# Two transformer blocks in sequence: residual with tokens on partitions, norms by token and by half of the tokens, gate/up/down interleaved, first product by k tiles

## The reference

```
for l in range(2):                                    # first block
    mod = silu(c) @ ada_w[l] + ada_b[l]               # shift, scale, gate for mixer and feed-forward
    h = rms_norm(x, g_pre_mix[l]) * (1.0 + scale_m) + shift_m
    proj = h @ w_in[l] + b_in[l]                      # 1024 -> 1280: q, k, v, u
    mix = concat([attention(q, k, v), pool(u)]) @ w_out[l]
    x = x + gate_m * rms_norm(mix, g_post_mix[l])
    h = rms_norm(x, g_pre_ffn[l]) * (1.0 + scale_f) + shift_f
    f = (silu(h @ w_gate[l]) * (h @ w_up[l])) @ w_down[l]      # 1024 -> 2816 -> 1024
    x = x + gate_f * rms_norm(f, g_post_ffn[l])
for l in range(2):                                    # second block
    z = rmsnorm(x, attn_norm[l]) @ w_in[l]            # split in 12 parts for the three mixers
    x = x + concat([y_a, y_b, y_c]) @ w_out[l]
    u = rmsnorm(x, ffn_norm[l]) @ ffn_w_up[l]
    x = x + (silu(causal_conv3(u[:, :FF])) * u[:, FF:]) @ ffn_w_down[l]
return rmsnorm(x, final_norm)
```

## Time and profile before

| | us |
|---|---|
| runs | 1308.36, 1308.45, 1309.59 |
| median | 1308.45 |
| span of the profiled execution | 1307.2 |
| TensorE busy | 1200.2 |
| VectorE busy | 878.0 |
| ScalarE busy | 625.0 |
| GpSimd busy | 30.2 |
| moved by DMA | 248.66 MB, 190 GB/s on average |

### The profile page before, as it was taken

How to read it: one execution, slowest core, us unless ns; L and a number is a source line. 1 busy time by engine, 2 the same in 40 slices (tenths; PEclk the granted TensorE clock), 3 DMA queues, 4 the chain that set the end, 5 groups by cost and what they waited for, 6 DMA issues and landing times.

```text
span 1307.2 us, 22230 instructions
## 1 busy us (share of the span) xinstructions
PE 1200.2 (92%) x9456; PEld 1154.1 (88%) x9456; DVE 878.0 (67%) x1355; ACT 625.0 (48%) x990; POOL 30.2 (2%) x32
## 2 busy tenths in 40 slices
PE   2589799989889899999899989999999998999997
PEld 1578699989878799999889789999989888999997
DVE  6697888876567566664377557888446655788743
ACT  2434544443345454453355556556435556555631
POOL 5400000000000000000000000000000000000000
PEclk9699999999989899999999999999999999999999
DMA  8863498887422345665243235556434423555630
GB/s 338 327 251 157 189 332 325 340 327 292 156 106 105 129 176 215 249 238 182 96 149 131 96 130 185 183 185 237 178 99 148 161 97 130 183 183 187 251 134 33
DMA packets 33570, 248.66 MB, mean 190 GB/s; under 512 B 3744, under 2 KB 4032, under 8 KB 6080
## 3 DMA queue, kind: packets, MB, share of 16 engines
q1 hardware_dynamic: 32400, 243.94, 51.3%
q10 hardware_dynamic: 720, 2.10, 0.4%
q0 software_dynamic: 352, 1.20, 0.4%
HBM read 246.18 MB, written 1.05 MB: 189 GB/s over the span
## 4 chain that ended last, share of the span: by engine, by line
PE 78%; DVE 12%; DMA 5%; ACT 5%; issue 1%; DVEq 0%; ACTq 0%
PE bank L440 24%; PE bank L442 23%; PE bank L441 23%; DMA raw_w<-weights 4%; DVE lo_w L1141 4%; PE bank L447 3%; DVE raw_w L1159 2%; PE bank L459 2%; ACT hi_w L867 2%; PE bank L748 2%; DVE raw L1168 1%; DVE prob L1218 1%; DVE smax L1221 1%; PE bank L728 1%; DMA c_row<-c 1%
## 5 line engine op out<-in xcount | busy, mean ns | idle before, releaser
L440 PE MATMUL bank<-in_hi,lo_w 128*128 128x256 f32 x1984 | 569.5, 287 | 43.5 <-DVE in_lo L1177 22.0
L1141 DVE TENSOR_TENSOR lo_w<-raw_w,hi_w 128x1024 fp32r<-128x1024 f32 (+4 forms) x344 | 426.0, 1279 | 205.1 <-ACT hi_w L867 205.0
L441 PE MATMUL bank<-in_lo,hi_w 128*128 128x256 f32 x1984 | 560.4, 282 | 0.0
L442 PE MATMUL bank<-in_hi,hi_w 128*128 128x256 f32 x1984 | 560.2, 282 | 0.0
L867 ACT ACTIVATE hi_w<-raw_w 128x1024 fp32r<-128x1024 f32 (+4 forms) x344 | 360.5, 1097 | 211.9 <-PE bank L442 177.9
L440 PEld LDWEIGHTS bank<-in_hi,lo_w 128*128 128x128 f32 x1984 | 379.8, 191 | 54.6 <-issue 39.7
L441 PEld LDWEIGHTS bank<-in_lo,hi_w 128*128 128x128 f32 x1984 | 380.4, 192 | 0.9 <-issue 0.5
L442 PEld LDWEIGHTS bank<-in_hi,hi_w 128*128 128x128 f32 x1984 | 379.8, 191 | 0.0
L440 PE MATMUL bank<-hid_hi,lo_w 128*128 128x256 f32 x704 | 200.1, 284 | 4.6 <-DVE hid_lo L1473 4.6
L442 PE MATMUL bank<-hid_hi,hi_w 128*128 128x256 f32 x704 | 198.0, 281 | 0.0
L441 PE MATMUL bank<-hid_lo,hi_w 128*128 128x256 f32 x704 | 198.0, 281 | 0.0
(11 more groups left out here) (174 smaller groups left out, 1121.1 us busy)
## 6 DMA issues: line engine op xcount, KB each, us to landing
raw_w<-weights SPq DMA_DIRECT2D x174, 1024.0 KB, 5.0
raw_w<-weights SPq DMA_DIRECT2D x32, 1408.0 KB, 6.1
raw_w<-weights SPq DMA_DIRECT2D x4, 1280.0 KB, 5.6
raw_w<-weights SPq DMA_DIRECT2D x8, 512.0 KB, 3.6
const<-const_table SPq DMA_DIRECT2D x1, 2434.0 KB, 13.1
raw_w<-weights SPq DMA_DIRECT2D x2, 1152.0 KB, 5.2
x<-x_t ACTq DMA_DIRECT2D x1, 1024.0 KB, 16.1
out_t<-raw SPq DMA_DIRECT2D x4, 256.0 KB, 2.5
```

The lines of the kernel that those rows point to most:

```text
L440: nc.tensor.matmul(o, st[1], mv[0], start=start, stop=False, **kw)
L441: nc.tensor.matmul(o, st[0], mv[1], start=False, stop=False, **kw)
L442: return nc.tensor.matmul(o, st[0], mv[0], start=False, stop=stop, **kw)
L1141: nc.vector.tensor_tensor(lo_w[:, m % NSPLIT, cut], raw_view(unit)[:, cut], hi_w[:, m % NSPLIT, cut].bitcast(F32), ALU.subtract).then_inc( ...
```

## The change

Everything is rewritten around a new layout of the residual; what is computed stays the same.

- `x` is now [128, 2, 1024]: tokens on partitions, in two halves T of 128 tokens. A norm is a sum along a row: ScalarE's square with an accumulated sum (`root`), with no matmul. The normed tokens go through TensorE as transposes (`turn_norm`, eight of 128x128 per half), and the high and low parts of the result are taken from PSUM. Gains, shifts and gates are now rows over all partitions; those of the modulation are computed as columns, written to memory and read back as rows by GpSimd (`mod_row`), which also multiplies by the scale row in three norms (`scale`).
- The out-projection and the down product have the activations stationary and 512 columns of weights moving (`into_y`). A `wd` unit is now two k tiles of all 1024 columns, 11 per layer, and the results stay in four banks of PSUM.
- A `wd` unit stands behind each pair of `gu` units (`ffn_units`), and only a ring of six hidden tiles is kept.
- A stage ends by halves (`ending`, `chain`): the last two units are finished for the first half of tokens, then for the second; the next stage's first two units are multiplied token half by token half (`front`), as soon as that half is normed. For gate/up these two units are turned back by eight transposes each.
- The input product of layer 0 goes by k tiles (`ink`, 128 rows of all 1280 columns), between the `ada` units that make shift and scale of the same tiles; the product takes six banks at once. In layers 0 and 1 q and k are rotated with tokens on partitions and then transposed; in layers 2 and 3 the same holds for the latents, and the unit `z` 2 has 208 columns in the place of padded and doubled blocks.
- `NSPLIT` is 3, raw slots have 2048 columns, and the `ada` units have other places.

```diff
-SLOT = FF
-NSPLIT = 2
+SLOT = 2048
+NSPLIT = 3
+RING = 6
...
+ADA_AFTER = {
+    ("wo", 0, 2): [(0, 8), (0, 9), (0, 10)], ("wo", 0, 3): [(0, 11), (0, 16), (0, 17)],
+    ("wo", 0, 0): [(0, 18), (0, 19), (0, 12)], ("wo", 0, 1): [(0, 13), (0, 14), (0, 15)],
+}
...
+def ffn_units(L):
+    lag = 1 if L < 2 else 2
+    units = []
+    for i in range(FT // 2):
+        units += [("gu", L, 2 * i), ("gu", L, 2 * i + 1)]
+        if i >= lag:
+            units.append(("wd", L, i - lag))
+    return units + [("wd", L, w) for w in range(WD - lag, WD)]
...
+    for j in range(4):
+        for n in (4 + j, j):
+            units.append((("ada", 0, n), *SHAPES["ada"]))
+        add("ink", 0, 2 * j)
+        add("ink", 0, 2 * j + 1)
...
-    def sums(N, tiles, ones, src, wait):
-        job = ("sums", *N)
-        b = take(job)
-        for i, t in enumerate(tiles):
-            wait(t)
-            last = nc.tensor.matmul(b[:, 0:256], ones, src[:, t, :], start=(i == 0), stop=(i == len(tiles) - 1))
-        last.then_inc(*sig(*job))
...
+    def turn_norm(N, T):
+        for c in range(2):
+            pe.wait_ge(*due("normed", N, T, c))
+            transposes(("tr", N, T, c), [normed[:, 512 * c + P * i:512 * c + P * (i + 1)] for i in range(4)])
...
+    def into_y(L, w, unit, T, first=False, last=False, before_second=None):
+        wait, slot, src = (mixed_wait, down_wait)[w](L)
+        wt = weights(unit, ("y", L, w, T, 1) if last else ("used", unit))
+        for c in range(2):
+            if c and before_second is not None:
+                before_second()
+            job = ("y", L, w, T, c)
+            if first:
+                take(job, 4 * w + 2 * T + c)
+            for n in range(2):
+                t = 2 * unit[2] + n
+                wait(t)
+                done = exact(ps(job)[:, :], [half(v_[:, slot(t), :], T) for v_ in src], [v_[:, n, cols(c)] for v_ in wt],
+                             start=(first and n == 0), stop=(last and n == 1))
+            if last:
+                done.then_inc(*sig(*job))
+        if T == 1 and not last:
+            done.then_inc(*sig("used", unit))
+    def ending(L, w, one, other, front):
+        N = after(L, w)
+        into_y(L, w, one, 0)
+        into_y(L, w, other, 0, last=True)
+        into_y(L, w, one, 1)
+        if N[0] == "final":
+            into_y(L, w, other, 1, last=True)
+            return
+        banks(*((4, 5, 6, 7) if w == 0 else (0, 1, 2, 3)))
+        if L >= 2:
+            into_y(L, w, other, 1, last=True, before_second=lambda: turn_norm(N, 0))
+        else:
+            into_y(L, w, other, 1, last=True)
+            turn_norm(N, 0)
+        front(0)
+        turn_norm(N, 1)
+        front(1)
...
+    def front(name, N, L, units):
+        def run(T):
+            job = (name, L, T)
+            b = take(job)
+            for i, u in enumerate(units):
+                done = tokens(two(b, i), u, ("used", u) if i == 0 else (name, L, 1), T,
+                              wait=lambda t: pe.wait_ge(*due("in_lo", N, T, t // 4)))
+                if i == 0 and T == 1:
+                    done.then_inc(*sig("used", u))
+            done.then_inc(*sig(*job))
+        return run
...
+            for kk in range(6):
+                for T, c in places:
+                    done = slice_of(kk, T, c)
+                done.then_inc(*sig("used", ("ink", 0, kk)))
...
+    def mod_row(L, kind, w):
+        n = ROWS[(L, kind, w)]
+        pool.wait_ge(*due("modcol", L, kind, w))
+        pool.dma_start(mod_rows[n, :].rearrange("(t p) -> p t", p=P), modcol[:, n, :], allow_slow_non_contiguous=True).then_inc(*sig("row_out", n, by=16))
+        pool.wait_ge(*due("row_out", n))
+        slot = ("gate", "scale", "shift").index(kind)
+        load(rows[:, slot, :], mod_rows[n:n + 1, :], D, f"row{slot}", L, kind, w)
...
+    def scale(N, L, w):
+        for T in range(2):
+            for c in range(2):
+                pool.wait_ge(*due("x", L, w, T, c))
+                if T == 0 and c == 0:
+                    pool.wait_ge(*due("row1", N[1], "scale", 0 if N[0] == "mix" else 1))
+                if T == 1:
+                    pool.wait_ge(*due("normed", N, 0, c))
+                nc.gpsimd.tensor_tensor(scaled[:, cols(c)], x[:, T, cols(c)], rows[:, 1, cols(c)], ALU.mult).then_inc(
+                    *sig("scaled", N, T, c))
...
+    def root(name, key, T, i, wait, src):
+        for c in range(2):
+            sc.wait_ge(*wait(c))
+            nc.scalar.activation(junk[:, :], src(c), ACT.Square, accum_out=ssq[:, T, c:c + 1]).then_inc(*sig("squared", *key, T, c))
+            if c == 0:
+                sc.wait_ge(*due("squared", *key, T, 0))
+                nc.scalar.activation(sbias[:, T, :], ssq[:, T, 0:1], ACT.Identity, bias=k("eps"), scale=1.0 / D).then_inc(*sig("sbias", *key, T))
+        sc.wait_ge(*due("sbias", *key, T))
+        sc.wait_ge(*due("squared", *key, T, 1))
+        r = tok_rstd[:, T, i:i + 1]
+        nc.scalar.activation(r, ssq[:, T, 1:2], ACT.Ln, bias=sbias[:, T, :], scale=1.0 / D).then_inc(*sig("mean_log", *key, T))
+        sc.wait_ge(*due("mean_log", *key, T))
+        nc.scalar.activation(r, r, ACT.Exp, scale=-0.5).then_inc(*sig(name, *key, T))
+    def chain(L, w, T, following):
+        N = after(L, w)
+        if L < 2:
+            root("rstd_post", (L, w), T, 0, lambda c: due("y", L, w, T, c), lambda c: ps(("y", L, w, T, c))[:, :])
+        root("rstd", (N,), T, 1, lambda c: due("x", L, w, T, c), lambda c: x[:, T, cols(c)])
+        if following is None:
+            return
+        prepare(following, (0,))
+        for c in range(2):
+            copy(("tr", N, T, c), in_hi[:, 4 * c:4 * c + 4, P * T:P * (T + 1)], by_tile(ps(("tr", N, T, c))), "in_hi", N, T, c, frees=False)
+        prepare(following, (1,))
...
+    def residual(L, w, T):
+        if L >= 2:
+            for c in range(2):
+                job = ("y", L, w, T, c)
+                ve.wait_ge(*due(*job))
+                nc.vector.tensor_tensor(x[:, T, cols(c)], x[:, T, cols(c)], ps(job)[:, :], ALU.add).then_inc(*sig("x", *job[1:], frees=job))
+            return
+        ve.wait_ge(*due("row0", L, "gate", w))
+        for c in range(2):
+            job = ("y", L, w, T, c)
+            ve.wait_ge(*due("squared", L, w, T, c))
+            if T == 1:
+                ve.wait_ge(*due("x", L, w, 0, c))
+            nc.vector.tensor_tensor(gained[:, cols(c)], ps(job)[:, :], rows[:, 0, cols(c)], ALU.mult).then_inc(*sig("gained", *job))
+        ve.wait_ge(*due("rstd_post", L, w, T))
+        for c in range(2):
+            job = ("y", L, w, T, c)
+            ve.wait_ge(*due("gained", *job))
+            nc.vector.scalar_tensor_tensor(x[:, T, cols(c)], gained[:, cols(c)], tok_rstd[:, T, 0:1], x[:, T, cols(c)], ALU.mult, ALU.add).then_inc(
+                *sig("x", *job[1:], frees=job))
+    def norm(N, T):
+        ve.wait_ge(*due("rstd", N, T))
+        r = tok_rstd[:, T, 1:2]
+        for c in range(2):
+            dst = final[:, T, cols(c)] if N[0] == "final" else normed[:, cols(c)]
+            if T == 1 and N[0] != "final":
+                ve.wait_ge(*due("tr", N, 0, c))
+            if N == ("mix", 0):
+                ins = nc.vector.tensor_scalar(dst, x[:, T, cols(c)], r, None, ALU.mult)
+            elif modulated(N):
+                ve.wait_ge(*due("scaled", N, T, c))
+                ve.wait_ge(*due("row2", N[1], "shift", 0 if N[0] == "mix" else 1))
+                ins = nc.vector.scalar_tensor_tensor(dst, scaled[:, cols(c)], r, rows[:, 2, cols(c)], ALU.mult, ALU.add)
+            else:
+                row, _ = norm_row(N)
+                ve.wait_ge(*due("row2" if N[0] == "ffn" else "row1", "norm", N))
+                ins = nc.vector.scalar_tensor_tensor(dst, x[:, T, cols(c)], r, row[:, cols(c)], ALU.mult, ALU.mult)
+            ins.then_inc(*sig("normed", N, T, c))
...
+    def chain(L, w, T, following):
+        N = after(L, w)
+        residual(L, w, T)
+        norm(N, T)
+        if following is None:
+            return
+        lo(following, (0,))
+        for c in range(2):
+            ve.wait_ge(*due("in_hi", N, T, c))
+            s_ = slice(P * T, P * (T + 1))
+            nc.vector.tensor_tensor(in_lo[:, 4 * c:4 * c + 4, s_], by_tile(ps(("tr", N, T, c))[:, :]), in_hi[:, 4 * c:4 * c + 4, s_].bitcast(F32),
+                                    ALU.subtract).then_inc(*sig("in_lo", N, T, c, frees=("tr", N, T, c)))
+        lo(following, (1,))
+        behind(following)
```

More of the change, by code:

```diff
@@ L38 @@
 POOLS = (2, 4, 8, 16)
-SLOT = FF
+SLOT = 2048
 NRAW = 3
-NSPLIT = 2
-NADA = 24
+NSPLIT = 3
+RING = 6
+PAIRED = [h for j in range(4) for h in (j, j + 4)]
 def const_table():
@@ L476, in product @@
                         wait(t)
+                    if between is not None and (i, t) == (1, 0):
+                        between()
                     c = c0 + P * i
                     kw = {} if wait is None or n == 1 else {"skip_group_check": True}
```

(49 more changed lines are left out.)

1940 lines of the change are left out of this document (1032 added, 908 removed).

## The result

The changed kernel takes 1289.2 us (median of four runs, 1284.4 to 1290.1), against 1308.9 us for the kernel before on the same chip: a ratio of 0.984 (95% interval 0.981 to 0.986). It is faster, by 19.6 us or 1.6%; forecast were 44 us. The profiled execution has a span of 1287.8 us.

What follows compares the result with a forecast made beforehand. The prediction took TensorE, busy 92% of 1307.2 us, as the bound. Stage times summed to 1248 us, plus 15 for the clock gave a 1263 span, and 1264 us kernel time, 44 less; range 1236 to 1291.

Steps and rivals of the forecast that it cites:

- the clock term: Six waits in layers 0 and 1, each followed by 2 to 3 us of half speed: 15 us added.
- Layer 0 to the input product of layer 1: From layer 0's out-projection to layer 1's input product: reached at 340 us, 363.3 before, including 14 us of stage-end waits.
- The upper bound of 24 us: Layer 0's shift row: longest assumed transfer through memory, four times pool_w's 6.1 us; the lower bound was 4.5.
- DMA stays under its rate: 312 GB/s: Gate/up/down stage: 5.2 MB in 16.8 us, where before held 309 GB/s without starving.
- TensorE's stream: Whole kernel: ones matmuls, rotations and padded columns go, 208 transposes come; net 41 us less work.
- 3 + 3.7: Stage ends in layers 0 and 1: TensorE waits 3 us for the first token half, 3.7 for the second.
- 306.7: Layers 2 and 3: us per layer, against 320.2 and 317.9 before; TensorE's last product ends at 1241.6.
- The 208 columns: Rival, unit z 2: 208-column steps fall back to plain fp32 at 0.365 us, 26 us more, 1289; chance 0.20.
- the fixed cost per matmul: Rival: 1536 wide steps replace 3072 narrow ones, saving 10 ns each; 15 us less, 1249; chance 0.04.
- The clock did not stay low: Answers a rival: split stage ends and softmax loops leave 1.2 GHz stretches, 108 us lost, 1356; chance 0.08.
- The cheap chains: Rival: waits in softmax, layer 0 and stage ends halve because ScalarE and VectorE overlap better; 1240; chance 0.10.
- The round trip rival: Rival, modulation row writes: 24 us instead of 5.4 each, layer 0's chain waits 19 longer; 1283; chance 0.06.

Runs made afterwards that it cites:

- fast writes: Against the changed kernel: modulation weights, biases and gains packed so each row is written in 32-byte runs and read in natural order; 1253.8 us, ratio 0.957.
- the run that was to confirm it: Against the changed kernel: rows read at once from the norm rows, 4-byte-element writes issued behind and not waited for until the last; 1295.8 us.

## Why the prediction was right and wrong

The starts of stages as forecast (without the clock term), in the kernel after, and in the one with fast writes:

| start of | forecast | after | fast writes |
|---|---|---|---|
| first product | 26 | 25.3 | 25.2 |
| out-projection, layer 0 | 104 | 111.5 | 110.4 |
| turned tokens, layer 0's stage end | 141 | 160.8 | 146.8 |
| input product, layer 1 | 340 | 372.2 | 345.0 |
| out-projection, layer 1 | 394.8 | 442.7 | 404.4 |
| first product, layer 2 | 625.2 | 665.2 | 627.9 |
| span | 1248 (+15) | 1287.8 | 1251.0 |

**The step that failed** is in "Layer 0 to the input product of layer 1": the row's way through memory at 5.4 + 4.5 us, taken near pool_w's 6.1 "with as many runs". pool_w is a read in runs of 512 bytes; its number of runs was like, their length was not. Measured: 9.0 to 15.4 us of waiting for the write, 8.4 for the read. The upper bound of 24 us held, but the rival made from it had only the latency in layer 0. Its 1283 lies near the measured 1289 by luck: most of the loss has another reason. Between the kernel after and the one with fast writes the span differs by 36.8 us: 1.0 before layer 0's out-projection, 13.0 from there to its first gate/up product (4.8 because the shift column is made later, its units having waited for transfers, 6.7 from the longer write, the rest from the read), 13.2 from there to layer 1's input product, 11.1 in layer 1's input product and attention, and -1.5 behind. So by the places where TensorE waits some 8 us are latency, which I had the form of, and about 28 are **disturbance of the weight transfers**, which the forecast had nowhere. That the writes in short runs cost 35 us is shown by the runs; the split into 8 and 28 is read from the traces, and the run that was to confirm it left the latency in the read. The sentence "DMA stays under its rate: 312 GB/s" was true of bytes: with fast writes this stage moves 301 GB/s and no wait of TensorE for weights is left in it. It said nothing of short writes on the same engines.

**What held.** TensorE's stream: 41 us less work forecast, 45 less busy, busy 1155.2 in the forecast's 1140 to 1160. First product at 25.3 (26). Layers 2 and 3 and the end, 622.6 (623). Layer 1's part from its out-projection to layer 2's first product, 222.5 (230.4): the forecast was too dear there, since the waits at its first stage end are 1.17 + 1.49 + 1.17 = 3.8 us and not 3 + 3.7. The 3 came from a chain "8.6 us" long, and the sum is wrong: without GpSimd's scalings and the transposes its parts are 9.0 us, with them over 13, and nothing says which of them overlap.

**Terms that were off and cancelled.** In the sum of layers 2 and 3 two times 306.7 from 625.2 end at 1238.6, where the text goes on with 1241.6; 306.7 holds one of the two stage ends of 3 us that the text names, and 1241.6 holds layer 2's other one. The start to layer 0's out-projection takes 6 to 7 us longer than 104, with VectorE waiting 7.9 us for rounded weights between 25 and 111 us, which my list of VectorE's work didn't have. The clock term of 15 us is not seen on top: with fast writes the span is 1251.0, 3 from the 1248 without it. Its granted clock in the windows is 0.98 in layer 0's gate/up/down stage and 0.88 in layer 1's attention, so some of the loss is there, and the smaller waits at stage ends will have paid for it. I can't split the two further, and that the sum without the clock comes so near is in part luck.

**The rivals.** The 208 columns (0.20) and the fixed cost per matmul (0.04) fall by the timeline of the kernel after. A step of 208 columns takes 0.11 us, not 0.365, and one of 512 still 0.23:

```profile
443.22 0.39 PE L476 MATMUL bank<-hi_w,in_hi 128*128 128x512 f32 x1
443.45 0.39 PE L474 MATMUL bank<-hi_w,in_lo 128*128 128x512 f32 x1
443.69 0.39 PE L475 MATMUL bank<-lo_w,in_hi 128*128 128x512 f32 x1
...
679.87 0.26 PE L474 MATMUL bank<-hi_w,in_lo 128*128 128x208 f32 x1
679.97 0.27 PE L475 MATMUL bank<-lo_w,in_hi 128*128 128x208 f32 x1
680.08 0.27 PE L476 MATMUL bank<-hi_w,in_hi 128*128 128x208 f32 x1
```

The Trainium skill's rule of a fixed cost per matmul ("TensorE: Matmul & The Clock Gate", section "Wait — 56ns, not 53.3ns?") is not borne out here: at a granted clock of 1.00 what lies above the columns at 2.4 GHz is 10 ns for 256 columns, 20 for 512 and 24 for 208. The 15 us that the prediction put beside this rule come from the 10 ns of the rows; by the figure of about 2.5 ns per matmul that this section of the Trainium skill gives, the estimate is 4 us. The clock did not stay low: 1.00 from layer 1's out-projection on. The cheap chains (0.10) were right for layer 1's first stage end, 3.8 us of waits in the place of 6.7, but even the kernel with fast writes ends at 1251 and not near their 1240. The round trip rival (0.06) was the right place at far too low a chance: it was the only term whose two bounds (4.5 and 24) lay a factor of five apart, and the rows could not narrow it.

## What to carry to other kernels

The price of a small write is set by its contiguous runs and not by its bytes: the same 4 KB in 1024 runs of 4 bytes or in 128 of 32. Whether the number of runs or their length counts, no run here separates; pool_w, a read in 1024 runs of 512 bytes, landed in 6.1 us in the kernel before and in 9.5 in the one after. The price is paid twice: by whoever waits for it, and by every large transfer on the same engines meanwhile. Look for a packing of data that is prepared beforehand (here weights and biases) that gives the small write its runs, before moving the stride to a consumer, where it cost another 18 us. Where a stage already asks for over 300 GB/s, bytes alone did not tell whether the DMA engines have room.

## What was new of the hardware

- A write of 4 KB in 1024 elements of 4 bytes is waited for 9.0 to 15.4 us and adds 6 to 8 us of all 16 DMA engines' time to the packets of the weights' queue; with 128 runs of 32 bytes it lands in 1.8 to 5.7 us and adds nothing that can be seen (664 us against 670 without writes). It is slow from GpSimd's queue and from SyncE's, where it lands in 9.7 to 12.8 us.
- Over 20 us with such writes the DMA engines are 91% busy at 192 GB/s, and 91% busy at 358 GB/s without one: their busy share did not tell how much they moved.
- A 208-column step costs 0.111 us, between the 0.095 in proportion to its columns and the 0.1165 of 256 columns, and like a transpose with 128.
- VectorE reads an fp32 operand with a stride of 8 elements at 1130 ns per 128x512 instead of 687 (tensor_tensor), and at 1623 instead of 957 (scalar_tensor_tensor).
